# Block 2's second convolution tile on ScalarE and GpSimd, head sums in two fp32r parts, gate rows picked by a matmul

## What is computed

```python
# block 1, per layer (cut)
q = rms_norm(q.reshape(b, s, 8, 64), q_norm_g)      # also k (2 heads) and the gated values (8 heads of 64)
# block 2, per layer (cut)
y = val * sigmoid(gate)                             # 256 channels: two tiles of 128
y = causal_depthwise_conv(y, dw) + dw_bias          # 31 taps, then a layer norm over the channels
beta = sigmoid(b);  g = -exp(a_log) * softplus(a + dt_bias)     # per token and head, 4 heads
g = cumsum(g per chunk)
decay = exp(g[i] - g[j]);  k_beta = k * beta;  ... a triangular solve per chunk and head
```

## Time and profile before

| what | us |
|---|---|
| median of 3 runs | 2551.18 (2549.28 to 2551.55) |
| the profiled execution | 2552.15 |
| its span in the trace | 2550.4 |
| TensorE matmuls busy | 2492.4 (98%) |
| VectorE busy | 1545.0 (61%) |
| ScalarE busy | 1094.3 (43%) |
| GpSimd busy | 227.2 (9%) |
| chain that ended last, TensorE's share | 88% |

### The profile page before, as it was taken

One profiled execution on the slowest core, in us unless ns is written; L12 is line 12 of the kernel. 1 busy time (PEld: TensorE's weight loads), 2 busy tenths in 40 slices (PEclk: granted clock), 3 DMA queues, 4 the chain that ended last, 5 costly groups with the idle time before them and its releaser, 6 DMA issues.

```text
span 2550.4 us, 36617 instructions
## 1 busy us (share of the span) xinstructions
PE 2492.4 (98%) x12846; PEld 1992.5 (78%) x12856; DVE 1545.0 (61%) x1994; ACT 1094.3 (43%) x1597; POOL 227.2 (9%) x186
## 2 busy tenths in 40 slices
PE   7999999999999999999999999999999999999998
PEld 5768888887668888887688778888776887788886
DVE  5766755757666736647986554344579865643444
ACT  4655423435554424433485442233334754431323
POOL 1010000000000000004212020000142120200000
PEclk9999999999999999999999999999999999999999
DMA  4203332333113333342120223233222202233333
GB/s 134 78 17 91 95 109 84 100 98 88 58 42 99 97 96 96 103 111 74 50 75 11 66 83 107 86 96 97 80 72 58 67 19 65 77 107 90 96 97 95
DMA packets 384483, 208.07 MB, mean 82 GB/s; under 512 B 9866, under 2 KB 380500, under 8 KB 384372
## 3 DMA queue, kind: packets, MB, share of 16 engines
q1 hardware_dynamic: 381284, 202.79, 27.5%
q0 software_dynamic: 2176, 3.06, 0.6%
q10 hardware_dynamic: 912, 0.77, 0.1%
HBM read 205.34 MB, written 2.10 MB: 81 GB/s over the span
## 4 chain that ended last, share of the span: by engine, by line
PE 88%; DVE 7%; ACT 2%; issue 1%; DMA 0%; POOL 0%; DVEq 0%; SPq 0%; ACTq 0%; POOLq 0%
PE ps L701 64%; PE ps L720 6%; PE ps L986 2%; DVE yc L2710 1%; DVE wlo L2276 1%; ACT whi L1564 1%; PE ps L1305 1%; PE ps L1164 1%; PE ps L1046 1%; PE ps L1048 1%; PE ps L1047 1%; PE ps L1176 1%; PE ps L1426 1%; PE ps L1428 1%; PE ps L1427 1%
## 5 line engine op out<-in xcount | busy, mean ns | idle before, releaser
L1564 ACT ACTIVATE whi<-raw 128x1024 fp32r<-128x1024 f32 (+1 forms) x354 | 395.8, 1118 | 989.4 <-PE ps L701 844.2
L701 PE MATMUL ps<-h_hi,whi 128*128 128x512 f32 x1920 | 761.8, 397 | 2.3 <-DVE za L2616 1.7
L701 PE MATMUL ps<-h_lo,whi 128*128 128x512 f32 x1920 | 750.0, 391 | 0.0
L701 PE MATMUL ps<-h_hi,wlo 128*128 128x512 f32 x1920 | 513.3, 389 | 0.0
L2276 DVE TENSOR_TENSOR wlo<-raw,whi 128x1024 fp32r<-128x1024 f32 (+1 forms) x354 | 467.0, 1320 | 64.2 <-ACT whi L1564 63.0
L701 PEld LDWEIGHTS ps<-h_hi,whi 128*128 128x128 f32 x1920 | 362.2, 189 | 84.3 <-issue 4.2
L701 PEld LDWEIGHTS ps<-h_lo,whi 128*128 128x128 f32 x1920 | 362.1, 189 | 78.7 <-issue 4.3
L701 PEld LDWEIGHTS ps<-h_hi,wlo 128*128 128x128 f32 x1920 | 360.5, 188 | 74.9
L701 PE MATMUL ps<-a_hi,whi 128*128 128x512 f32 x592 | 230.3, 389 | 0.0
L701 PE MATMUL ps<-a_lo,whi 128*128 128x512 f32 x592 | 230.3, 389 | 0.0
L3039 DVE TENSOR_TENSOR cv<-ps,rstd 128x512 f32<-128x512 f32 x80 | 55.3, 692 | 228.7 <-PE ps L701 228.7
(11 more groups left out here) (429 smaller groups left out, 3427.0 us busy)
## 6 DMA issues: line engine op xcount, KB each, us to landing
raw<-in_w_up SPq DMA_DIRECT2D x128, 512.0 KB, 3.8
raw<-in_w_down SPq DMA_DIRECT2D x64, 704.0 KB, 4.5
raw<-in_w_in SPq DMA_DIRECT2D x82, 512.0 KB, 3.8
raw<-in_w_gate SPq DMA_DIRECT2D x40, 512.0 KB, 3.8
raw<-in_w_o SPq DMA_DIRECT2D x16, 512.0 KB, 3.6
raw<-in_w_out SPq DMA_DIRECT2D x16, 512.0 KB, 3.7
xs<-in_x SPq DMA_DIRECT2D x2, 1024.0 KB, 6.8
raw<-in_w_gate SPq DMA_DIRECT2D x8, 256.0 KB, 2.8
```

What stands on the lines that cost most here:

```text
L701: return pe.matmul(ps[:, ACC[s], :], w[s][:, k, :], r[:, k, :], start=start, stop=stop)
L1564: act.activation(whi[s][:, 0:kt, :], raw[s][:, 0:kt, :], ACT.Copy).then_inc(w_hi_ready.sem, 1)
```

## The change

**Sums of squares, block 1.** GpSimd splits each square into two fp32r parts (`square_split`); TensorE sums both with an fp32r copy of `blk`, one unit later than before, in four banks. `rs`, norm, rotary and low halves move one unit later. Two products of fp32r a tile take the place of one of f32.

```diff
+                def square_split(j):                       # GpSimd, after the square of tile j
+                    nc.gpsimd.tensor_copy(sq_hi[:, j % 4, :], square).then_inc(sq_split.sem, 1)
+                    pool.wait_ge(sq_split.sem, sq_split.at(L, 2 * j))
+                    nc.gpsimd.tensor_tensor(sq_lo[:, j % 4, :], square, sq_hi[:, j % 4, :].bitcast(F32), ALU.subtract).then_inc(sq_split.sem, 1)
...
+                def square_sums(j):                        # TensorE
+                    bank = ps[:, (STAT + ROT)[j % 4], :]
+                    pe.wait_ge(sq_split.sem, sq_split.at(L, 2 * j + 1))
...
+                    pe.matmul(bank, blk_r[:], sq_hi[:, j % 4, :], start=True, stop=False)
+                    pe.matmul(bank, blk_r[:], sq_lo[:, j % 4, :], start=False, stop=True)\
...
-                    pe.matmul(ps[:, STAT[i % 2], :], blk[:], msq[:, i % 2, :], start=True, stop=True).then_inc(qkstat_ready.sem, 1)
...
-                    if i - 2 <= NQ:
-                        head_sums(i - 2)
+                    if 0 <= i - 3 <= NQ:
+                        square_sums(i - 3)
```

```diff
+    SIDE = {**{10 + p: (2 * p, 2 * p + 1) for p in range(8)}, **{18 + n: (16 + n,) for n in range(4)}}
+    SIDE_IN = 20
...
+                def tap_product(k):                        # ScalarE, step i, after the exponentials
...
+                    if k >= 3:
+                        act.wait_ge(late_tapped.sem, late_tapped.at(L, k - 3))
+                    order.told(act.activation(dst, ypad[:, 1, k:k + SEQ], ACT.Identity, bias=bias, scale=param(pd, L, D_DW + k * NC + 1)),
+                               tap_scaled, L, k)
...
+                def side_tap(k):                           # GpSimd, step i, after that step's counted()
+                    pool.wait_ge(tap_scaled.sem, tap_scaled.at(L, k))
+                    if k > 0:
...
+                        nc.gpsimd.tensor_tensor(yc[:, 1, :], yc[:, 1, :], msq2[:, k % 2, :], ALU.add)\
+                            .then_inc((late_tapped if k < CT - 1 else dw_ready).sem, 1)
...
                 def taps(k0, k1):
                     for k in range(k0, k1):
                         order.settle()
-                        for t in range(NC):
...
+                            ins = dve.scalar_tensor_tensor(yc[:, 0, :], src, w, yc[:, 0, :], ALU.mult, ALU.add)
...
-                    if n in (0, 1):                        # ScalarE, beside level n of the solve
-                        act.wait_ge(kk_ready.sem, kk_ready.at(L, GH - 2 + n))
-                        tap_product(n)
-                    if 2 <= n - 2 < CT - TAPS_IN:
-                        act.wait_ge(late_tapped.sem, late_tapped.at(L, n - 4))
-                        tap_product(n - 2)
+                    if n < CT - SIDE_IN:
+                        tap_product(SIDE_IN + n)
```

```diff
+                    if i == 12:
+                        decay_sums()
+                    if i == 13:
+                        turn_gate_parts()
...
+                    if kt == 0 and h == 1:
+                        pe.wait_ge(rows_kept.sem, rows_kept.at(L, 0))
...
-                    for tb in range(TB):
-                        mm = pe.matmul(ps[:, ROT[0], tb * P:(tb + 1) * P], cols["g"][:, tb, h:h + 1].to_broadcast([P, P]),
-                                       tri[:], start=True, stop=True)
-                    mm.then_inc(grow_ready.sem, 1)
+                    n = 4 * GH
+                    pe.matmul(ps[:, ROT[0], :], gate_pick[0:n, h:h + 1].to_broadcast([n, P]), gate_rows[0:n, :],
+                              start=True, stop=True).then_inc(grow_ready.sem, 1)
...
+                def decay_columns():                       # VectorE, end of step 12
...
+                    for n, name in enumerate(("gc", "beta")):
+                        order.step(dve.tensor_copy(gate_split[:, :, 2 * n * GH:(2 * n + 1) * GH], cols[name][:]))
+                    order.settle()
+                    for n, name in enumerate(("gc", "beta")):
...
+                        ins = dve.tensor_tensor(gate_split[:, :, lo], cols[name][:], gate_split[:, :, hi].bitcast(F32), ALU.subtract)
...
+                    if i == 13:                            # VectorE, end of step 13
+                        dve.wait_ge(gate_turned.sem, gate_turned.at(L, 0))
+                        order.told(dve.tensor_copy(gate_rows[0:4 * GH, :], ps[0:4 * GH, TRN[1], :]), rows_kept, L, 0)
```

More of the change, by code:

```diff
@@ L147, in network @@
         rstd = sb("rstd", [P, SEQ])
+        with ExitStack() as before_ssq:
+            gate_rows = before_ssq.enter_context(nc.sbuf_tensor("gate_rows", [P, SEQ], F32R))
         ssq = sb("ssq", [P, SEQ])
@@ L293, in network @@
             kr = [sb("kr0", [P, SEQ], F32R, on=on)]
+            with ExitStack() as before_vvT:
+                sq_lo = sb("sq_lo", [P, TB, SEQ], F32R, on=before_vvT)
             vvT = sb("vvT", [P, TB, SGW], on=on)
@@ L304, in network @@
             u = sb("u", [P, NS, SEQ], on=on)
+            with ExitStack() as before_ao:
+                sq_hi = sb("sq_hi", [P, TB, SEQ], F32R, on=before_ao)
             ao = sb("ao", [P, NQ, SEQ], on=on)
             rope = sb("rope", [P, 2, SEQ], on=on)
-            perm = sb("perm", [P, P], on=on)
+            blk_r = sb("blk_r", [P, P], F32R, on=on)
             sgb = sb("sgb", [P, NS, P], on=on)
@@ L388, in setup_tables @@
         def setup_tables():
-            for dst, name in ((blk, "c_blk"), (perm, "c_perm")):
-                yield dst[:], D[name]
+            yield blk[:], D["c_blk"]
             yield rope[:], D["c_rope"].rearrange("a p n -> p a n")
@@ L575, in mixer_added @@
                         .then_inc(osq_used.sem, 2 if i % NS == 1 else 1)
+                def square_split(j):
+                    if j <= NQ:
+                        pool.wait_ge(qksq_ready.sem, qksq_ready.at(L, j))
+                    else:
+                        pool.wait_ge(vvsq_ready.sem, vvsq_ready.at(L, j - NQ - 1))
+                    if j >= 4:
+                        pool.wait_ge(qkstat_ready.sem, qkstat_ready.at(L, j - 4))
+                    square = msq[:, j % 2 if j <= NQ else (j - NQ - 1) % 2, :]
+                    nc.gpsimd.tensor_copy(sq_hi[:, j % 4, :], square).then_inc(sq_split.sem, 1)
+                    pool.wait_ge(sq_split.sem, sq_split.at(L, 2 * j))
+                    nc.gpsimd.tensor_tensor(sq_lo[:, j % 4, :], square, sq_hi[:, j % 4, :].bitcast(F32), ALU.subtract).then_inc(sq_split.sem, 1)
+                    pool.wait_ge(sq_split.sem, sq_split.at(L, 2 * j + 1))
+                for j in range(NQ + 1):
+                    square_split(j)
                 added_last = {4: (L, 3), 7: (L, NS + 1)}
@@ L583, in _ @@
                     query_beside(h)
+                    if h == 1:
+                        pool.wait_ge(qm_ready.sem, qm_ready.at(L, h))
+                        for j in range(NQ + 1, NQ + 1 + NS):
+                            square_split(j)
                     if h in (3, 6, 7):
@@ L1977, in _ @@
                                 exponentials(h, kt)
+                    for k in SIDE.get(i, ()):
+                        tap_product(k)
                     if i in (15, 18):
@@ L2320, in _ @@
                     keep_rows(*ROW_TURNS[n - 4])
+            dve.wait_ge(setup_loaded.sem, SETUP)
+            order.step(dve.tensor_copy(blk_r[:], blk[:]))
             order.restart()
@@ L2597, in _ @@
                     low(V + 2, 0, KD)
+                    for n in range(2):
+                        of = [ident[:, (2 * n + e) * GH:(2 * n + e + 1) * GH] for e in range(2)]
+                        order.step(dve.tensor_tensor(gate_pick[:, n * GH:(n + 1) * GH], of[0], of[1], ALU.add))
                 dve.wait_ge(rstd_ready.sem, rstd_ready.at(G, 0))
```

157 lines of the change are left out of this document (77 added, 80 removed).

## The result

The changed kernel takes 2562.22 us (median of 6 runs, 2559.13 to 2564.23) against 2551.22 (6 runs, 2549.28 to 2551.55). The ratio is 1.0042, 95% interval 1.0029 to 1.0054: slower by 11 us, where 2537 was predicted. The profiled execution took 2559.22 us for a span of 2557.4, so it shows 7.0 of the 11 us. The kernel's own runs spread over 5 us, and the longest has a mean granted clock of 0.989 where the profiled one has 0.994.

A forecast was written before the change was run, and what follows sets the result against it. TensorE, busy for 98% of the span, was taken to bound the kernel. -7.4 - 6.8 - 3.8 + 3.6 = -14.4 us, from 2552.15 profiled to 2537.7; median 1.0 under: 2537, eight-in-ten range 2526 to 2550.

The forecast's parts named there:

- part 1: Block 1, sums of squares as two fp32r products: -3.7 us a layer, -7.4 in all (between -8.2 and -4).
- part 3: Block 2, second convolution tile to ScalarE and GpSimd: 2.8 us wait for row maxima goes; -6.8 us (0 to -11).
- part 4: Block 2's head units, gate rows by two fp32r products a head: 1.9 us a layer, -3.8 in all.
- part 5: The solve, eleven tap additions on GpSimd in place of eight: +1.8 us a layer, +3.6 in all (0 to +5).
- Part 2: Price of a GpSimd addition on VectorE: 0.72 x 0.64 = 0.45 us, with ends 0 and 0.72.
- 0 to 1 us late: Block 2 after unit 13: VectorE's lateness when TensorE comes to the first gate wait, for the turned parts.
- 0.4 to 1 us early: Block 2 after unit 14: TensorE comes this early to its wait for VectorE's gate rows, ahead of head 1's values.
- (b): Block 2 part wins nothing, GpSimd giving VectorE back what it took (0.72 against 0.715): 2543.5 or 2550; chance 0.24.
- (c): Block 2, units 10 to 17: additions block VectorE their whole time, 1.27 us in place of 0.45: 2562; chance 0.07.
- deciding point: (c) decides from 0.83 us an addition, 14.4 / 2 / 19 = 0.38 above the forecast's price.
- no wait of TensorE for GpSimd's parts: Sign in block 1: unit and sum 5.9 us apart, TensorE never waiting for the split squares.
- half clock in units 12 to 16: Block 2: a sign named in advance that would show the forecast wrong.

The follow-up runs named there:

- p4: The kernel before with only the gate rows changed, decay sums after unit 20, parts turned after unit 21, rows awaited at head 0; 2546.65 us, ratio 0.9985.
- e13: The whole change with ScalarE's products beside the solve, from the third on, issued two steps later; 2562.16 us, ratio 1.0042.
- e5: The changed kernel with GpSimd's 19 additions a layer beside units 10 to 21 cut to 8 of 512 columns, waits kept; 2543.86 us, ratio 0.9972.

## Why the prediction was wrong

The forecast was some 14 us faster and the change is 11 us slower. In the terms of the sum, by the profiled execution, part 1 missed by 7.3 us, part 3 by 10.8, part 4 by 2.5 and part 5 by 1.9. Less the 1.0 us of the earlier start that makes 21.5, the distance from the sum of -14.4 to the 7.0 us of the trace. What failed in the main is that the prediction had GpSimd's parts of the squares and VectorE's gate parts and gate rows ready, or nearly, when TensorE asks for them.

**Part 1, -7.4: measured 0.** The price of a sum was right (0.39 saved a sum, 0.455 predicted). The step that failed is that the parts would be ready when TensorE asks: 3.2 us a square were set against 5.9 us a unit, but the gated values' sums are asked for two a unit. GpSimd took 0.6 to 1.5 us for a cast and 1.3 to 2.1 for a subtraction, and cost 1.8 us, with the half clock behind it in six of seven profiled executions. The second miss is that ScalarE's steps "a unit later" were costed at nothing; what stands behind them in its queue lost 0.9. The 0.4 us for a low half were right.

**Part 2, 0.45 us an addition.** Measured 0.66 for the additions' work, within the ends of 0 and 0.72 but near the upper, and 0.79 against the low halves of before, above both. The estimate spread the price over all of a step's VectorE time; in fact the additions met mostly two-input work out of SBUF. Row maxima and drains, which read PSUM, took the same beside them (1216 and 690 ns in the change against 1215 and 691 before).

**Part 3, -6.8: measured +0.7 in the projections and +3.3 on the way to the heads.** The stall at the earlier trace rows went as said. "0 to 1 us late" at the gate parts was 2.2 in both layers, and "0.4 to 1 us early" at the rows was 1.9 late in the first. The layout priced an addition by a mean of 0.45 us, but it is a whole low half that is stretched, from 1.22 us to 2.0 in the mean and 2.31 just there. The wait behind ScalarE at head 0 I had only as a lost gain; it came ahead of the gate rows with 1.6 us, so that what TensorE gained in the projections was waited away there for ScalarE, which is the last to be ready.

**Part 4, -3.8: measured -1.3** in the change and -5.9 where the rows stand alone (p4). The mechanism is right, its cover was named, and what the heads gave back (0.8 us at the keys, 1.2 at the turned blocks, a clock of 0.95 in the earlier trace rows's third stretch) was 1.3 us a layer more than counted.

**Part 5, +3.6: measured +5.5,** above the upper end of +5. The mechanism is right, and the wait ahead of a level, by ScalarE's queue, came with 1.9 us in place of 1.0 and a clock of 0.83 behind it. Undone (e13), it comes back at the mean.

**The rivals.** (b) was nearest as a mechanism: GpSimd's additions give VectorE back about what the moved taps took (0.66 to 0.79 against 0.715 a tap). But it kept the gains of block 1 and of the heads. (c)'s time is the one that came, by another sum, so its 2562 was luck: its price of 1.27 us did not occur as a mean. Its deciding point, 0.83, starts from the sum of -14.4, of which block 1 brought nothing, and counts only VectorE's load and not the two gate waits. With these a price under it was enough: without the additions' work the change takes 2543.9 (e5). Two places show what the price is made of. The low half at 1230.12 came while one addition was under way and another stood behind: the three, undisturbed, would take 1.27 + 1.22 + 1.27 = 3.76 us one after another, and took 3.94 (1229.61 to 1233.55). That is as if only one of the two engines worked at a time; but the addition that had begun first, by its row here, was stretched too:

```profile
1229.61 1.74 POOL L700 TENSOR_TENSOR yc<-yc,sqt 128x512 f32<-128x512 f32 x1
```

The second took 2.06 us, so each side pays a part, and an addition in these units takes 1.66 us in the mean. Three short taps, 2.33 us undisturbed, and two products, 2.49 beside such taps, took 3.65 together, and 3.77 in the kernel before (GpSimd's row begins within VectorE's):

```profile
1226.55 3.65 DVE L2752 SCALAR_TENSOR_TENSOR gq<-zp,pd,gq 128x512 f32<-128x512 f32 x3
```

```profile
1226.83 2.83 POOL L664 TENSOR_TENSOR probs<-probs,times 128x512 f32<-128x512 f32 x2 [4.97 <-ACT probs L1930]
```

The Trainium skill ("SBUF — State Buffer", section "Summary: rules for kernel authors", on running VectorE and GpSimd at once) says that the later engine "fully blocks". The total at the first place agrees with it, the 1.74 us of the engine that had begun doesn't, nor does the second place (3.65 against 4.82 us one after another, or 4.66 with the shortest product, 1.16). In neither does VectorE pay the whole of each GpSimd operation, as I had read the rule in (c): the low half took 1.09 us more beside two additions, the taps 1.32 more beside two products.

Of the signs named in advance, no stall at unit 11 and VectorE over 90% busy came; "no wait of TensorE for GpSimd's parts" was wrong, the waits of up to 1 us in units 13 and 14 were 2.2 and 1.9, and the one ahead of the mean stood ahead of a level instead. Of the signs of being wrong, the queries' short taps were stretched by 0.37 us in the mean (1126 against 752 ns), not by 0.83, but half clock in units 12 to 16 was there, in the second layer:

```profile
1942.00:1952.00 10.00, 9.01 (x31) 6.72 (x33) 9.30 (x15) 2.50 (x5) 3.01 (x4) 0.66 0.20 52
```

## What to carry to other kernels

Before work is moved from an engine that is late now and then to others, spread it where it is: one line that moved four multiply-adds out of the critical units did what 20 products on ScalarE and 19 additions on GpSimd a layer could not. A side engine's work is to be laid against the operations that run in its very microseconds and what stands behind them in the queue, not against a stage's mean load. And a short chain between engines belongs where each has room, not just after its inputs are ready.

## What the runs showed of the hardware

GpSimd's 128x512 additions out of SBUF and VectorE's two-input operations slow each other: low halves went from 1.29 to 2.03 us in the mean (1.22 undisturbed, 1.94 to 2.32 for the nine of ten that met GpSimd's work), additions from 1.27 to 1.66. Operations of VectorE that read PSUM are not stretched. Half clock after a wait of about 2 us is not certain: behind block 1's wait for GpSimd it came in the first layer in six of seven profiled executions and in the second in none, and the change's own was the seventh. The change, which adds such waits, has the wider spread (5.1 us between its runs, 2.3 before), and one trace of it can miss a part of its cost. GpSimd's cast of 128x512 took 0.61 us at its shortest and its subtraction 1.29, and up to 1.5 and 2.1 beside VectorE's work, while VectorE's cast of a 128x16 tile took 0.95 us beside an addition of GpSimd, with which it ended, and 0.16 without it.
